# Attention scores over 64 rows of the TensorE array, two head groups issued as a pair, on one Trainium2 core

## Chip, core and metric

The kernel runs on one core of one Trainium2 chip. The metric is the device time in microseconds (us) of one execution. Three timed runs of the kernel before gave a median of 1534.31 us, from 1533.08 to 1535.16. The profile comes from one further execution, which took 1534.36 us.

## What is computed

The reference is a hybrid attention layer followed by a retention and feed-forward layer, on 512 tokens of 1024 features, all in float32. The change touches only the attention of the first layer: a local branch with a window of 128 tokens (8 heads, called A), and a selected and a window branch (8 heads, called B). With 512 tokens the top 16 of 8 blocks are all blocks, so the selected branch is causal attention over everything, and the window of 512 is too. Each branch has 8 query heads of 64 features in two groups; the four heads of a group share one key and one value head:

```python
logits = jnp.einsum('btgrd,bsgd->bgrts', qi, kb) + bias      # d = 64
p = masked_softmax(logits, mask, sink)
return jnp.einsum('bgrts,bsgd->btgrd', p, vb)
```

The compressed branch, the gates, the projections and the second layer are the same before and after.

## The kernel before

`proj` holds the projections with features on the 128 partitions and the 512 tokens along the free dimension. One tile of queries, `proj[:, QA + j]` or `proj[:, QB + j]`, holds two heads: head j of group 0 on partitions 0 to 63 and head j of group 1 on partitions 64 to 127. The keys of a branch lie in the same way, group 0 on the low and group 1 on the high half. A product of queries and keys is taken over all 128 rows. So that the other group adds nothing, the kernel keeps two copies of each key tile with one half set to zero: `k_group0[branch]` has group 0 and zeros on the high half, and the tile in `proj` itself (KA, KS or KW) keeps group 1 with zeros on the low half. These copies are made in VectorE's `head_norm` for t >= 8 (lines 1111 to 1120), with the high halves zeroed at n == 20 (line 1149). KC and VC are tiles whose contents are no longer needed by then; `ka0` is a tile of its own.

The attention is a loop over 96 steps, written out on each engine (`for s in range(STEPS)`; line 1784 on TensorE, 1206 on VectorE, 811 on ScalarE). `Step` gives what step s does: the query block i runs from 0 to 3, in it the branch from 0 to 2, and in that eight heads, j and g with g fastest, so steps s and s+1 with s even are the same j, block and branch, in groups 0 and 1. The width of the scores is 128 times the number of key blocks: i + 1 for the branches 1 and 2, and at most 2 for branch 0. Counting these gives 24 steps of width 128, 40 of 256, 16 of 384 and 16 of 512.

A step goes through the engines like this. TensorE computes the scores of step s into bank s % 2 (called QK(s) below; line 1792). VectorE adds the bias and finds the row's minimum, into `sc[:, s % 2]` (bias(s); line 1217). ScalarE takes the exponential in place (exp(s); line 818). TensorE transposes the result block by block (T(s); line 1817, recorded as line 1571), VectorE for even and ScalarE for odd s copy it out of PSUM (lines 1231, 827), and TensorE multiplies with the values (PV(s); line 1806). On TensorE the order in iteration s of the loop is: wait for bias(s-2), QK(s); PV(s-3); T(s-1), which waits for exp(s-1). VectorE's bias(s) waits for QK(s) and, since it writes `sc[:, s % 2]`, for T(s-2). VectorE also closes each group of eight steps, with its three operations at lines 1241 to 1260.

A float32 product appears in the trace as two instructions LDWEIGHTS and two MATMUL, each with its own weights and both into the same bank; a transpose is one of each. Ahead of the loop lies the computation of the z projections, units n = 16 to 23 (line 1701), with the head norms between, and the compressed branch (lines 1748 to 1781). After the loop TensorE waits for `yl_done` and goes on to the output projection.

Of the kernel before, what the change touches and what calls it, by code (L numbers as in the profile page):

```python
# [28 lines left out]
ALU = mybir.AluOpType  # L29
AX = mybir.AxisListType.X  # L30

P = 128
S = 512
# [5 lines left out]
HD = 64  # L39
# [11 lines left out]
KC, VC, KS, VS, KW, VW, KA, VA, QA, QB, ZA, ZB = 0, 1, 2, 3, 4, 5, 6, 7, 8, 12, 16, 20  # L51
# [46 lines left out]
N_ATT = 8 * N_GROUPS  # L98
# [21 lines left out]
def att(s):  # L120
    return Step(s)


def tail_at(s):

    i, rest = divmod(s - 5, 24)
    return i - 1 if rest == 0 and i > 0 else None
# [36 lines left out]
def hybrid_block(nc, x, c, w_ada, b_ada, norm_gain, w_in, b_nsa_gate, q_gain_a, k_gain_a, sinks,  # L164
# [7 lines left out]
    with ExitStack() as stack:  # L172
# [3 lines left out]
        def sb(name, shape, kb, dt=F32):  # L176
            return nc.alloc_sbuf_tensor_at(name, shape, dt, offset=BASE + int(kb * KB))

        def sem(name):
            return stack.enter_context(nc.semaphore(name))  # L180
# [7 lines left out]
        def const(name, shape, dt=F32):  # L188
            t = sb(name, shape, c_at[0] / KB, dt)
            c_at[0] += (int(np.prod(shape[1:])) * 4 + 31) // 32 * 32  # L190
            return t
# [11 lines left out]
        gains = const("gains", [P, 6])  # L203
# [31 lines left out]
        R = 60  # L235
# [22 lines left out]
        h_hi = sb("h_hi", [P, KT, S], R + 48, F32R)  # L258
        h_lo = sb("h_lo", [P, KT, S], R + 64, F32R)
        proj = sb("proj", [P, 24, S], R + 80)  # L260
        ka0 = sb("k_local_group0", [P, S], R + 128)
        rs_bc = sb("rstd_wide", [P, 2, S], R + 40)
        gb_t = sb("gates_t", [P, S], R + 44)
        hid = sb("cmp_hidden", [P, 2, 64], R + 130.25)
# [71 lines left out]
        ps = nc.alloc_psum_tensor("ps", [P, 8, S], F32)  # L336
# [17 lines left out]
        m = {n: sem(n) for n in names}  # L354
# [1 line left out]

        nrm = {n: sem(n) for n in ("x_done xh_done xl_done xsq_done ss_done nst_mm ms_done rs_done nbc_mm rb_done t_done h_done l_done").split()}


        k_group0 = (ka0[:], proj[:, KC], proj[:, VC])  # L360

        def gate_of(branch):

# [623 lines left out]
        def _(dve):  # L987
            v = nc.vector
            own = Own(dve, m["dve_own"])
# [67 lines left out]
            for u in range(U_KA, U_Z):  # L1057
# [10 lines left out]
                if c is not None:  # L1068
                    dve.wait_ge(ada_in[c], 64 + 16)
                    for k in (2 * c, 2 * c + 1):  # L1070
# [5 lines left out]
                        if k and k % 2 == 0:  # L1076
                            dve.wait_ge(m["adag_done"], c)
                        ins = v.scalar_tensor_tensor(out=acc_g[:], in0=src, scalar=csilu[:, k:k + 1],
                                                     in1=acc_g[:], op0=ALU.mult, op1=ALU.add)
# [26 lines left out]
            def head_norm(t):  # L1106

                dve.wait_ge(m["bc_mm"], t + 1)
                tile = proj[:, NORM_TILES[t]]
                g = NORM_GAINS[t]  # L1110
                if t >= 8:

                    low, high = slice(0, HD), slice(HD, P)
                    own(v.scalar_tensor_tensor(out=k_group0[t - 8][low, :], in0=tile[low, :], scalar=gains[low, g:g + 1],
                                               in1=ps[low, 5 + t % 2], op0=ALU.mult, op1=ALU.mult))
                    v.scalar_tensor_tensor(out=tile[high, :], in0=tile[high, :], scalar=gains[high, g:g + 1],
                                           in1=ps[high, 5 + t % 2], op0=ALU.mult, op1=ALU.mult).then_inc(m["qk_done"], 1)
                    own.wait()
                    own(v.memset(tile[low, :], 0.0))
                    return  # L1120
                v.scalar_tensor_tensor(out=tile, in0=tile, scalar=gains[:, g:g + 1], in1=ps[:, 5 + t % 2],
                                       op0=ALU.mult, op1=ALU.mult).then_inc(m["qk_done"], 1)

# [4 lines left out]
            for n in range(16, 24):  # L1128
                dve_convert(dve, None, 0, n + U_OF + AHEAD)
                if n < 19:  # L1130
                    a, b = NORM_GROUPS[n - 16]
                    dve.wait_ge(m["st_mm"], b)
                    v.tensor_scalar(msq_h[:, 8 * a:8 * b], ps[:, 4, 8 * a:8 * b], EPS, None, ALU.add).then_inc(m["hms_done"], 1)
                if n == 17:
                    cmp_input(1)
                    dve.wait_ge(m["kst_mm"], 1)
                    v.tensor_scalar(kc_ms[0:NC_PAD, :], ps[0:NC_PAD, 7, 448:450], EPS, None, ALU.add).then_inc(m["kms_done"], 1)
                if n == 19:
                    dve.wait_ge(m["kbc_mm"], 1)
                    own(v.memset(kcz[:], 0.0))  # L1140
                    own.wait()
                    for g in range(2):
                        half = slice(g * HD, (g + 1) * HD)
                        v.scalar_tensor_tensor(out=kcz[half, g], in0=kcmp[half, :], scalar=gains[half, 3:4],
                                               in1=ps[half, 7, 480:512], op0=ALU.mult, op1=ALU.mult).then_inc(m["kcmp_done"], 1)
                if n == 20:
                    own(v.memset(vbd[:], 0.0))
                    for k0 in k_group0:
                        own(v.memset(k0[HD:P, :], 0.0))
                for t in BCAST_AT.get(n, ()):  # L1150
                    head_norm(t)
                if n == 22:

                    dve.wait_ge(m["c2_mm"], 2)
                    own.wait()
                    for g in range(2):
                        for j in range(4):
                            part = slice(32 * j, 32 * j + 32)
                            v.tensor_copy(vbd[part, g, j * HD:(j + 1) * HD],
                                          ps[part, 7, 320 + g * HD:384 + g * HD]).then_inc(m["vbd_done"], 1)  # L1160
# [45 lines left out]
            for s in range(STEPS):  # L1206
                if s < N_ATT:
                    u = att(s)
# [16 lines left out]
                t = s - 1  # L1225
# [131 lines left out]
            for t in range(KT):  # L1357
# [6 lines left out]
                for k in MIX_TILES[t]:  # L1364
# [10 lines left out]
                                           op0=ALU.mult, op1=ALU.add))  # L1375
                own.wait()
                own(v.scalar_tensor_tensor(out=conv_t[:], in0=u_pad[:, 2:S + 2], scalar=tap[2], in1=conv_t[:],
                                           op0=ALU.mult, op1=ALU.add))
# [94 lines left out]
            for h in range(RET_HEADS):  # L1473
                for n in range(6):
# [9 lines left out]
                    if n == 5:  # L1484
# [8 lines left out]
                        for t in range(4):  # L1493
                            c1 = V_RET + 4 * h + t
                            own(v.scalar_tensor_tensor(out=val[:], in0=ret[:, 4 * h + t], scalar=col[:, c1:c1 + 1],
                                                       in1=ps[:, 6], op0=ALU.mult, op1=ALU.mult))
# [9 lines left out]
            with dve.Fori(0, 2) as it:  # L1506
                own.begin(it, 4)
                for k in range(8):
                    dve_convert(dve, it, 8, U_YR + k + AHEAD)
                    if k % 2:  # L1510
                        t = k // 2
# [43 lines left out]
            for k in range(3 * KT):  # L1555
                t, part = divmod(k, 3)
# [12 lines left out]
        def _(pe):  # L1569
            def trans(dst, src, parts=P):  # L1570
                return pe.transpose(dst, src, ident[0:parts, 0:parts])  # L1571

            def blk(i):
                return slice(i * P, (i + 1) * P)
# [207 lines left out]


            for s in range(STEPS):
                if s < N_ATT:
                    u = att(s)
                    if s >= 2:
                        pe.wait_ge(m["s_bias"], s - 1)

                    q = (QB if u.branch else QA) + u.j  # L1790
                    keys = proj[:, (KA, KS, KW)[u.branch]] if u.g else k_group0[u.branch]
                    pe.matmul(ps[:, s % 2, 0:u.width], proj[:, q, blk(u.i)],  # L1792
                              keys[:, u.first_block * P:u.first_block * P + u.width],
                              start=True, stop=True).then_inc(m["s_mm"], 1)
                t = s - 3
                if 0 <= t < N_ATT:
                    u = att(t)
                    pe.wait_ge(m["pt_a" if t % 2 else "pt_d"], t // 2 + 1)
                    if t == 0:
                        pe.wait_ge(m["co_done"], NI)  # L1800
                    elif t % 8 == 0 and u.group >= 2:
                        pe.wait_ge(m["comb_done"], u.group - 1)
                    v, blocks = (VA, VS, VW)[u.branch], u.width // P
                    for b in range(blocks):
                        c = (u.first_block + b) * P + u.g * HD
                        mm = pe.matmul(ps[:, 4 + u.group % 2, u.head * HD:(u.head + 1) * HD], pt[:, t % 2, blk(b)],  # L1806
                                       proj[:, v, c:c + HD], start=b == 0, stop=b == blocks - 1)
                    mm.then_inc(m["pv_mm"], 1)
                t = s - 1
                if 0 <= t < N_ATT:  # L1810
                    pe.wait_ge(m["s_exp"], t + 1)
                    if t == 0:
                        pe.wait_ge(m["ctr_mm"], 1)
                    if t >= 2:
                        pe.wait_ge(m["pt_a" if t % 2 else "pt_d"], t // 2)
                    for b in range(att(t).width // P):
                        mm = trans(ps[:, 2 + t % 2, blk(b)], sc[:, t % 2, blk(b)])
                    mm.then_inc(m["t_mm"], 1)
                i = tail_at(s)
                if i is not None:  # L1820
                    pe.wait_ge(m["ob_done"], 2 * i + 2)
                    pe.wait_ge(m["comb_done"], 3 * i + 3)
                    if i:
                        pe.wait_ge(m["yf_done"], 2 * i)
                    for half, o in enumerate((oa, ob[:, i])):
                        for b in range(4):
                            mm = trans(ps[:, 6 + half, blk(b)], o[:, blk(b)])
                    mm.then_inc(m["ytr_mm"], 1)
# [101 lines left out]
            with pe.Fori(0, 2) as it:  # L1930
                for k in range(8):
                    half = k % 2
# [18 lines left out]
            with pe.Fori(0, 2) as it:  # L1951
                for k in range(12):
                    t, part = divmod(k, 3)
# [74 lines left out]
```

## Time and profile before

| | us |
|---|---|
| median of three timed runs | 1534.31 |
| the profiled execution | 1534.36 |
| its span in the trace | 1532.6 |
| TensorE matmul busy | 1481.7 |
| VectorE busy | 744.9 |
| ScalarE busy | 576.0 |
| GpSimd busy | 85.7 |
| the attention loop, from its first to its last score or transpose | about 245.9 to 377.9 |

Times in the trace count from the start of the span, which is 1.8 us shorter than the execution. PE is the matmul side of TensorE and PEld its weight loads. The start of a matmul is recorded; its end is modelled and takes in the way through the array, so neighbouring matmuls overlap in the rows and the distance of two starts tells what one costs in a stream.

### The profile page before, as it was taken

What the parts mean: (1) busy time and instruction counts of PE and PEld (TensorE: products, weight loads), DVE (VectorE), ACT (ScalarE), POOL (GpSimd) and SP (SyncE); (2) the same over time, 40 slices, a digit from 0 to 9 for tenths busy, and PEclk for the clock granted to TensorE, in tenths of its full rate; (3) what the DMA queues carried; (4) which work ended last, traced back from release to release, by engine and by line L of the source; (5) the groups of instructions that cost most, each with busy time, mean ns of one, the idle gap of its engine ahead of it and who ended that gap; (6) DMA issues with size and microseconds to landing.
All of it is one profiled execution on the core that took longest, in us unless ns stands there. A gap on an engine that the chain in (4) does not pass through costs nothing.

```text
span 1532.6 us, 18206 instructions
## 1 busy us (share of the span) xinstructions
PE 1481.7 (97%) x7006; PEld 1233.1 (80%) x7006; DVE 744.9 (49%) x1205; ACT 576.0 (38%) x949; POOL 85.7 (6%) x90
## 2 busy tenths in 40 slices
PE   5899997998999999999999999999999999999998
PEld 4688886887888888888888878878878888888886
DVE  5743156875556653454544525554456533333332
ACT  3432335654433333233333334442345433333221
POOL 1110400000000000001000022210000000000000
PEclk9997899999999999999999999999999999999998
DMA  7992310000252333322221223225333323232321
GB/s 230 277 267 73 107 56 15 2 1 1 83 165 86 107 105 96 100 84 68 70 83 56 82 60 93 83 83 165 92 88 94 107 87 109 87 106 87 113 76 55
DMA packets 227757, 145.51 MB, mean 95 GB/s; under 512 B 6082, under 2 KB 216250, under 8 KB 227424
## 3 DMA queue, kind: packets, MB, share of 16 engines
q1 hardware_dynamic: 224784, 131.90, 29.6%
q0 software_dynamic: 2896, 12.57, 2.9%
q8 instruction: 50, 0.82, 0.2%
q14 instruction: 27, 0.22, 0.0%
HBM read 138.82 MB, written 4.59 MB: 94 GB/s over the span
## 4 chain that ended last, share of the span: by engine, by line
PE 69%; issue 24%; DVE 3%; SPq 2%; ACT 1%; DMA 0%; POOLq 0%; POOL 0%; DVEq 0%; ACTq 0%
PE ps L381 44%; PE ps L1872 6%; PE ps L1896 3%; PE ps L1670 3%; PE ps L1792 3%; PE ps L1571 3%; PE ps L1806 3%; PE ps L1882 1%; PE ps L1693 1%; SPq L479 1%; PE ps L1686 1%; SPq L501 1%; SPq L515 1%; DMA w_raw<-in_w_in_dram 0%; PE ps L1780 0%
## 5 line engine op out<-in xcount | busy, mean ns | idle before, releaser
L399 DVE TENSOR_TENSOR w_lo<-w_raw,w_hi 128x1024 fp32r<-128x1024 f32 (+1 forms) x215 | 261.2, 1218 | 245.4 <-ACT w_hi L394 242.7
L394 ACT ACTIVATE w_hi<-w_raw 128x1024 fp32r<-128x1024 f32 (+1 forms) x215 | 220.4, 1034 | 24.2 <-PE ps L381 12.8
L431 ACT ACTIVATE temps<-ps 128x512 f32<-128x512 f32 x68 | 40.6, 597 | 251.1 <-PE ps L381 251.1
L381 PE MATMUL ps<-g_hi,w_hi 128*128 128x512 f32 x384 | 97.4, 396 | 0.0
L381 PE MATMUL ps<-g_hi,w_lo 128*128 128x512 f32 x384 | 94.9, 389 | 0.0
L381 PE MATMUL ps<-g_lo,w_hi 128*128 128x512 f32 x384 | 94.8, 389 | 0.0
L381 PEld LDWEIGHTS ps<-g_hi,w_hi 128*128 128x128 f32 x384 | 71.6, 188 | 16.4 <-issue 1.9
L381 PEld LDWEIGHTS ps<-g_hi,w_lo 128*128 128x128 f32 x384 | 72.1, 188 | 15.1
L381 PEld LDWEIGHTS ps<-g_lo,w_hi 128*128 128x128 f32 x384 | 72.1, 188 | 15.0
L1806 PEld LDWEIGHTS ps<-proj,probs_t 128*128 128x128 f32 x432 | 61.4, 191 | 13.9 <-issue 7.6
L818 ACT ACTIVATE scores_sb<-scores_sb,row_min 128x256 f32<-128x256 f32 (+3 forms) x96 | 51.2, 533 | 54.3 <-DVE row_min L1217 53.3
L381 PE MATMUL ps<-f_hi,w_hi 128*128 128x512 f32 x288 | 71.1, 389 | 0.0
L381 PE MATMUL ps<-f_hi,w_lo 128*128 128x512 f32 x288 | 71.1, 389 | 0.0
L381 PE MATMUL ps<-f_lo,w_hi 128*128 128x512 f32 x288 | 71.1, 389 | 0.0
L381 PEld LDWEIGHTS ps<-f_hi,w_lo 128*128 128x128 f32 x288 | 54.1, 188 | 11.2
L381 PEld LDWEIGHTS ps<-f_hi,w_hi 128*128 128x128 f32 x288 | 54.1, 188 | 11.2
L381 PEld LDWEIGHTS ps<-f_lo,w_hi 128*128 128x128 f32 x288 | 54.1, 188 | 11.2
L1806 PE MATMUL ps<-proj,probs_t 128*128 128x64 f32 x432 | 58.6, 263 | 0.0
L1792 PE MATMUL ps<-proj 128*128 128x256 f32 (+3 forms) x160 | 53.8, 418 | 0.0
L628 POOL TENSOR_TENSOR rstd<-mean_squares,minus_half 128x4 f32<-128x4 f32 x8 | 8.2, 1023 | 766.4 <-DVE mean_squares L1300 733.0
L1282 DVE TENSOR_TENSOR x_t<-temps,x_t 128x512 f32<-128x512 f32 x16 | 11.1, 692 | 81.9 <-ACT temps L431 81.9
L1571 PE MATMUL ps<-ident,scores_sb 128*128 128x128 f32 x224 | 42.8, 284 | 6.3 <-ACT scores_sb L818 6.0
(368 smaller groups left out, 2740.1 us busy)
## 6 DMA issues: line engine op xcount, KB each, us to landing
w_raw<-in_w_in_dram SPq DMA_DIRECT2D x107, 512.0 KB, 3.8
w_raw<-in_w_ff_gate_dram SPq DMA_DIRECT2D x22, 512.0 KB, 3.8
w_raw<-in_w_ff_up_dram SPq DMA_DIRECT2D x22, 512.0 KB, 3.8
w_ada_shift_scale<-in_w_ada_dram SPq DMA_DIRECT2D x16, 512.0 KB, 6.7
w_raw<-in_w_r_out_dram SPq DMA_DIRECT2D x16, 512.0 KB, 4.6
w_raw<-in_w_ff_down_dram SPq DMA_DIRECT2D x16, 512.0 KB, 4.2
w_ada_gate<-in_w_ada_dram SPq DMA_DIRECT2D x4, 1024.0 KB, 9.2
w_raw<-in_w_out_dram SPq DMA_DIRECT2D x8, 512.0 KB, 4.0
```

Of the source, the lines that this page charges most:

```text
L381: mm = pe.matmul(bank, w[:, slot, k], mov[:, at_k], start=first and n == 0 and k == 0, stop=last and n == 2 and k == kts - 1)
L394: act.activation(whi[:, slot, 0:kts], raw[:, slot, 0:kts], ACT.Copy).then_inc(hi_done, 1)
L399: nc.vector.tensor_tensor(wlo[:, slot, 0:kts], raw[:, slot, 0:kts], whi[:, slot, 0:kts].bitcast(F32), ALU.subtract).then_inc(lo_done, 1)
L431: act.activation(dst, ps[:, o % 4], func, scale=scale).then_inc(evac, 1)
L479: sp.dma_start(ada[:, u % 4, :, part], w_ada_v[:, :, n:n + P]).then_inc(ada_in[u % 4], 16)
L818: a.activation(sc[:, s % 2, 0:w], sc[:, s % 2, 0:w], ACT.Exp, scale=-1.0, bias=row_min[:, G % 2, n:n + 1], accum_out=den[:, G % 2, att(s). ...
L1571: return pe.transpose(dst, src, ident[0:parts, 0:parts])
L1670: mm = pe.matmul(ps[:, 4 - 4 * q + j], half_rows(w, u)[:, kk, blk(j)], h[:, 2 * c2 + kk], start=c2 == 0 and n == 0 and kk == 0, stop=c2 == ...
L1792: pe.matmul(ps[:, s % 2, 0:u.width], proj[:, q, blk(u.i)], keys[:, u.first_block * P:u.first_block * P + u.width], start=True, stop=True). ...
L1806: mm = pe.matmul(ps[:, 4 + u.group % 2, u.head * HD:(u.head + 1) * HD], pt[:, t % 2, blk(b)], proj[:, v, c:c + HD], start=b == 0, stop=b = ...
L1872: mm = pe.matmul(ps[:, 4 + j], x[:, 2 * c2 + kk, blk(j)], half_rows(w, u)[:, kk], start=c2 == 0 and n == 0 and kk == 0, stop=c2 == 3 and n ...
L1896: mm = pe.matmul(ps[:, 4 + t], w[:, j, blk(t)], p[:, j], start=n == 0 and j == 0, stop=n == 2 and j == NI - 1)
```

## The change

The key tiles are no longer split: `head_norm` handles them as it handles the query tiles, with one operation over 128 partitions, and the copies, their zeroing and the tile `ka0` go away. The score products now take only the 64 partitions of their group, for queries and keys. On TensorE the scores of steps s and s+1 are issued one right after the other at the even s, each behind its wait for the bias two steps before it; at odd s none are issued.

```diff
-        ka0 = sb("k_local_group0", [P, S], R + 128)
-        k_group0 = (ka0[:], proj[:, KC], proj[:, VC])
...
-                if t >= 8:
-
-                    low, high = slice(0, HD), slice(HD, P)
-                    own(v.scalar_tensor_tensor(out=k_group0[t - 8][low, :], in0=tile[low, :], scalar=gains[low, g:g + 1],
-                                               in1=ps[low, 5 + t % 2], op0=ALU.mult, op1=ALU.mult))
-                    v.scalar_tensor_tensor(out=tile[high, :], in0=tile[high, :], scalar=gains[high, g:g + 1],
-                                           in1=ps[high, 5 + t % 2], op0=ALU.mult, op1=ALU.mult).then_inc(m["qk_done"], 1)
-                    own.wait()
-                    own(v.memset(tile[low, :], 0.0))
-                    return
                 v.scalar_tensor_tensor(out=tile, in0=tile, scalar=gains[:, g:g + 1], in1=ps[:, 5 + t % 2],
                                        op0=ALU.mult, op1=ALU.mult).then_inc(m["qk_done"], 1)
...
                     own(v.memset(vbd[:], 0.0))
-                    for k0 in k_group0:
-                        own(v.memset(k0[HD:P, :], 0.0))
...
             for s in range(STEPS):
-                if s < N_ATT:
-                    u = att(s)
-                    if s >= 2:
-                        pe.wait_ge(m["s_bias"], s - 1)
-
-                    q = (QB if u.branch else QA) + u.j
-                    keys = proj[:, (KA, KS, KW)[u.branch]] if u.g else k_group0[u.branch]
-                    pe.matmul(ps[:, s % 2, 0:u.width], proj[:, q, blk(u.i)],
+                for e in (s, s + 1) if s < N_ATT and s % 2 == 0 else ():
+                    u = att(e)
+                    if e >= 2:
+                        pe.wait_ge(m["s_bias"], e - 1)
+
+                    q, half = (QB if u.branch else QA) + u.j, slice(u.g * HD, u.g * HD + HD)
+                    keys = proj[half, (KA, KS, KW)[u.branch]]
+                    pe.matmul(ps[:, e % 2, 0:u.width], proj[half, q, blk(u.i)],
                               keys[:, u.first_block * P:u.first_block * P + u.width],
                               start=True, stop=True).then_inc(m["s_mm"], 1)
```

## Rows read from the trace of the kernel before

**Rows 1.** The page's busy time of each engine: us, share of the span, instructions.
```profile
PE 1481.7 (97%) x7006; PEld 1233.1 (80%) x7006; DVE 744.9 (49%) x1205; ACT 576.0 (38%) x949; POOL 85.7 (6%) x90
```

**Rows 2.** Stretches of the loop: length, busy of PE, PEld, DVE, ACT, POOL, clock, DMA.
```profile
250.00:262.00 12.00, 9.72 (x76) 8.44 (x76) 7.69 (x45) 8.07 (x40) 0.00 (x0) 1.00 0.01 3
...
344.00:358.00 14.00, 14.00 (x92) 10.65 (x89) 7.31 (x20) 7.63 (x18) 0.00 (x0) 1.00 0.01 2
```

**Rows 3.** Timeline of PE: start, length, engine, line, operation; scores of neighbouring steps.
```profile
289.01 0.60 PE L1792 MATMUL ps<-proj 128*128 128x256 f32 x2
290.06 0.60 PE L1792 MATMUL ps<-proj 128*128 128x256 f32 x2
...
346.33 1.02 PE L1792 MATMUL ps<-proj 128*128 128x512 f32 x2
348.47 1.02 PE L1792 MATMUL ps<-proj 128*128 128x512 f32 x2
```

**Rows 4.** Timeline, single instructions of one step of width 512, on PE.
```profile
350.51 0.27 PE L1571 MATMUL ps<-ident,scores_sb 128*128 128x128 f32 x1
350.62 0.59 PE L1792 MATMUL ps<-proj 128*128 128x512 f32 x1
351.05 0.59 PE L1792 MATMUL ps<-proj 128*128 128x512 f32 x1
```

**Rows 5.** Timeline of a narrow step (width 128), from one stalled transpose to the next.
```profile
249.27 0.33 PE L1571 MATMUL ps<-ident,scores_sb 128*128 128x128 f32 x1 [0.38 <-ACT scores_sb L818]
249.43 0.39 PE L1792 MATMUL ps<-k_local_group,proj 128*128 128x128 f32 x2
249.86 0.35 DVE L1217 CUSTOM_DVE_ANT_0 scores_sb<-ps,band_a,sinks_negated 128x128 f32<-128x128 f32 x1
250.25 0.40 ACT L818 ACTIVATE scores_sb<-scores_sb,row_min 128x128 f32<-128x128 f32 x1 [0.49 <-DVE row_min L1217]
250.80 0.33 PE L1571 MATMUL ps<-ident,scores_sb 128*128 128x128 f32 x1 [0.26 <-ACT scores_sb L818]
```

**Rows 6.** Timeline around two products on a part of the array, ahead of the loop.
```profile
76.32 0.26 PE L1571 MATMUL ps<-ident,vec 110*128 110x110 f32 x1
76.51 0.14 PEld L1571 LDWEIGHTS ps<-ident,vec 32*128 32x128 f32 x1 [0.28 <-issue]
...
190.69 0.39 PE L381 MATMUL ps<-h_lo,w_hi 128*128 128x512 f32 x1
191.01 0.10 PEld L1571 LDWEIGHTS ps<-ident,k_compressed_rstd 32*64 32x64 f32 x1 [0.35 <-issue]
191.01 0.21 PE L1571 MATMUL ps<-ident,k_compressed_rstd 32*64 32x32 f32 x1
191.15 0.13 PEld L1581 LDWEIGHTS ps<-ident,k_compressed_rstd 32*64 32x64 f32 x1
191.23 0.22 PE L1581 MATMUL ps<-ident,k_compressed_rstd 32*64 32x32 f32 x1
191.37 0.15 PEld L1571 LDWEIGHTS ps<-ident,rstd_wide 128*128 128x128 f32 x1
```

**Rows 7.** Timeline: a float32 product whose weights could not be loaded ahead.
```profile
240.62 0.19 PEld L1780 LDWEIGHTS ps<-v_compressed_diagonal,probs_t 128*128 128x128 f32 x1 [2.19 <-issue]
240.65 0.45 PE L1780 MATMUL ps<-v_compressed_diagonal,probs_t 128*128 128x256 f32 x1 [1.98 <-DVE probs_t L1192]
240.94 0.38 PE L1780 MATMUL ps<-v_compressed_diagonal,probs_t 128*128 128x256 f32 x1
```

**Rows 8.** Timeline of DVE: what the split of one key tile costs.
```profile
218.28 0.74 DVE L1114 SCALAR_TENSOR_TENSOR k_local_group<-proj,gains,ps 64x512 f32<-64x512 f32 x1 [10.98 <-PE ps L1571]
219.06 0.75 DVE L1116 SCALAR_TENSOR_TENSOR proj<-proj,gains,ps 64x512 f32<-64x512 f32 x1
219.97 0.48 DVE L1119 MEMSET proj<- 64x512 f32 x1 [0.16 <-issue]
```

**Rows 9.** Waits from 180 to 246 us: the only one of PE for DVE.
```profile
PE ps L1780 <- DVE probs_t L1192: 2.0, 1, 2.0
```

## The prediction

> **What bounds the kernel now.** I read the page's engine totals first: TensorE is busy for 97% of the span [rows 1], so the question is whether it is also full where the change acts. The change acts in the attention loop, 132 of 1534 us. The stretches of the loop show two regimes [rows 2]: with blocks of scores 512 wide, PE is busy for 14.00 of 14.00 us; with blocks 128 wide, for 9.72 of 12.00 us.
>
> In the full regime the distance of the score products is the cost of a step: 1.05 us at width 256 and 2.14 at 512 [rows 3]. Within a step, a score instruction of width 512 starts 0.43 us before the next, so the two of a product take 0.86, and a transpose takes 0.11 [rows 4]. That is the rate of all of it: an instruction takes its width x 0.43/512 us, but not under 0.11, which is what its load of 128 columns of weights takes. A product of width w so costs 0.21 us per 128 columns; width 256: scores 0.43, four value instructions 0.43, two transposes 0.21, sum 1.07 against 1.05 seen.
>
> In the narrow regime a chain sets the pace [rows 5]: transpose 249.27, scores 249.43, bias 249.86, exponential 250.25, next stalled transpose 250.80: 1.53 us for two steps, with PE waiting at its end for ScalarE.
>
> **The change part by part.** *Split of the keys.* For each of three key tiles VectorE loses 0.74 + 0.75 + 0.48 and gains one operation over 128 partitions, which takes as long as one over 64 at the same width, say 0.74 [rows 8]; with three fills of 0.48 that is 3 x 1.23 + 1.4 = 5 us less of VectorE's work between 195 and 229 us. I cost it at nothing: the one wait of PE for VectorE in that stretch is 2.0 us for another operation, at 240.6, which follows from products of PE that end after these [rows 9]. If that cover were missing, it could give at most those 5 us.
>
> *Where the halves of the array could save.* By the code, 12 pairs of steps have width 128, 20 have 256, 8 have 384 and 8 have 512. A score product keeps its width, so over 64 rows it costs the same 0.21 us per 128 columns; what can be won is overlap of the two groups. No row shows two products side by side. The ends are no overlap (four units of the cost of one instruction per pair, as now) and full overlap (two units). I take three, for this reason: each product is two MATMULs with their own weights on the same rows, so the two of one group can't overlap, and in all rows MATMULs start in the order of the program. Then group 1's first can start with group 0's second at the earliest, and its second is alone. One unit of four is saved: per pair 0.21 at 256, 0.32 at 384, 0.43 at 512. At 128 I count nothing, since four weight loads of 0.11 fill that time anyway. Over the pairs in the full regime: 20 x 0.21 + 8 x 0.32 + 8 x 0.43 = 10.2 us.
>
> *What switching costs.* All else in the loop uses the whole array, so each pair enters and leaves another shape of it. The rows of three such entries and exits agree [rows 6]. The first weight load of the new shape starts 0.07 us before the modelled end of the matmul before it and no earlier: 76.32 + 0.26 - 0.07 = 76.51; 190.69 + 0.39 - 0.07 = 191.01; and out, 191.23 + 0.22 - 0.08 = 191.37. In one shape it is loaded during the matmul before. A float32 product with weights not loaded ahead begins late by that load: 240.94 less its cost of 0.21 is 240.73, or 0.11 us after the load at 240.62 [rows 7]. In: from the last transpose's start 0.27 - 0.07 + 0.11 = 0.31 instead of 0.11, so 0.20 more [rows 4]. Out: the last score instruction takes 0.59 by its row where it costs 0.43 [rows 4]; 0.59 - 0.07 + 0.11 = 0.63 instead of 0.43, again 0.20. A round trip is 0.40 us. The nearest lower bound is the trip at 76 us, about 0.27, where the load is that of a transpose; the lowest is zero, if 64 rows are not such a shape. The Trainium skill, page "TensorEngine Tiling (Array Packing)", section "Key Properties", says that a change of tiling mode drains TensorE; the trace agrees, with the 0.32 us from 190.69 to 191.01.
>
> In the full regime 36 trips cost 36 x 0.40 = 14.4. In the narrow one the chain passes only through the entry (transpose, then scores); the exit falls in the time in which PE waits for the exponential. 12 x 0.20 = 2.4.
>
> *Order and waits.* Scores of s+1 now come ahead of PV(s-3) and T(s-1), behind the wait for bias(s-1). Queued behind that wait are those two, and ScalarE and VectorE wait for them. bias(s-1) waits for T(s-3), which ends well before: at width 256, from there to QK(s+1) PE has PV 0.43, T 0.21, the entry 0.20 and QK(s) 0.43, 1.27 us in all, for one bias. Closing a group may delay one in eight a little, as it does now. The other chain, from the end of QK(s) to T(s), has 0.43 + 0.21 + 0.43 + 0.43 = 1.50 us of PE work now and 0.21 + 0.20 + 0.43 + 0.21 + 0.43 = 1.48 after. I cost the order at nothing; what hides it is that PE work, and at width 256 it has little to spare.
>
> **The sum**, against the profiled execution of 1534.36 (the median, 1534.31, is the same): + 14.4 + 2.4 - 10.2 = + 6.6 us, 1541.0. By width, in us a pair: + 0.20 at 128, + 0.19 at 256, + 0.08 at 384, - 0.03 at 512.
>
> **Rivals.**
> *A, the switch is free* (64 full-width rows are no new shape, or the drain needs nothing). Then only the 10.2 us remain: 1524.2, faster. Against it: three entries and exits of three shapes all drained. For it: none of them was 64 x 128. It decides the sign where a round trip costs under 10.2 / 42 = 0.24 us (36 full trips and 12 halves), and 0.27 is the lowest seen.
> *B, full overlap* (two units). Saves 20.5 instead of 10.2, with the switch as forecast: 1530.7. Against it: the order of MATMULs and the two of each product.
> *C, no overlap*: four units as now, with the switch: 1534.4 + 16.8 = 1551.2. For it: the trace shows no two products at once, ever.
> *D, each half drains too*: going from one part of the array to another, the load at 191.15 came 0.21 - 0.07 = 0.14 after the matmul at 191.01, where 0.05 would do, though the shape was the same [rows 6]. Then there is no overlap, and per full pair one more drain of 0.20: 1551.2 + 36 x 0.20 = 1558.4. For it: that row; against it: there both parts shared their rows, here they don't. The Trainium skill, page "TensorE: Matmul & The Clock Gate", section "The mechanism", says that weight loads overlap with matmuls in flight only on other rows, and that matmuls start in order. By the first, this rival would fall and the forecast's overlap stand; no row shows either half of it for these halves.
>
> **How the numbers follow.** Forecast 1541 with chance 0.45 (its own range 1537 to 1545, for a trip between 0.31 and 0.50 us), A 0.13, B 0.10, C 0.17, D 0.10, and 0.05 for something else, such as a lower clock: the loop's stretches had 1.00 even where PE was busy for only 9.72 of 12 us [rows 2]. The range for 8 in 10 leaves out A and the unnamed rest: from 1529, below B, to 1560, above D. About 0.2%, or 3 us, is what a measurement of this kernel can tell from no change. Faster by more: A, half of B and a little of the rest, 0.20. Within: half of B, and the forecast's case with a trip near the low bound of 0.27, 0.14. Slower: 0.66.
>
> **What would show it.** In the timeline after, the first weight load of a pair stands about 0.20 us behind the last transpose's start, and that of the values 0.52 behind the last score instruction at width 512; if they are pulled ahead, A holds. The start of group 1's first MATMUL equals that of group 0's second if there is overlap, that of group 0's first if B holds, and lies a unit behind it for C. A pair at 512 takes 4.26 us (now 4.28), at 256 about 2.3 (now 2.1), at 128 about 1.73 (now 1.53). The stage ahead of the loop keeps its length though VectorE is busy 5 us less. Idle time of PE at width 256 that ends with the exponential or the bias would mean that the order costs after all; a clock under 1.00 in the loop would break all of it.

## The result

The changed kernel takes 1541.11 us (median of 20 runs), the kernel before 1535.14 (20 runs): a ratio of 1.0046, 95% interval 1.0030 to 1.0061. That ratio is one of means, over all but the slowest run of the changed kernel: two of its twenty took 1561.54 and 1563.29, with an average clock of 0.954 where the others have 0.969 to 0.972. The medians alone give 1.0039, or 6.0 us more. I had forecast 6.6 more, 1541.0. The number is right, but two terms of its sum were wrong and cancelled, which is luck: the overlap of the two halves saves two of the four units of a pair and not one, and in the profiled run the clock of TensorE fell for 30.7 us, which I had given a small chance.

### The profile after

In the changed kernel the scores are line 1777, the values 1791, the transposes 1556, bias 1202, exponential 815. The engine totals of its page (us, share of the span, instructions) answer to [rows 1]:

```profile
span 1539.3 us, 18197 instructions
PE 1490.7 (97%) x7006; PEld 1226.6 (80%) x7006; DVE 740.1 (48%) x1196; ACT 577.6 (38%) x949; POOL 85.6 (6%) x90
```

VectorE does 4.8 us less, in 9 instructions fewer, as the removed copies should give; PE is busier by 9 us. The stretches of the loop (columns as in [rows 2]) show where:

```profile
250.00:262.00 12.00, 11.65 (x61) 9.05 (x60) 6.47 (x34) 7.09 (x31) 0.00 (x0) 0.60 0.01 2
262.00:274.00 12.00, 11.94 (x54) 8.85 (x55) 6.45 (x32) 6.87 (x27) 0.00 (x0) 0.50 0.00 1
284.00:296.00 12.00, 11.49 (x85) 8.42 (x84) 9.03 (x34) 8.46 (x29) 0.00 (x0) 1.00 0.00 0
358.00:372.00 14.00, 14.00 (x102) 10.29 (x102) 8.62 (x22) 7.60 (x18) 0.00 (x0) 1.00 0.01 2
```

The column before the last two is the granted clock. It is 0.50, the 1.2 GHz level, at 262 to 274 us, and 1.00, 2.4 GHz, from 284 us on. PE "busy" for 11.94 of 12 us there did only 54 matmuls. In the kernel before, the clock is 1.00 both at 250 to 262 us [rows 2] and in the stretch after it, with 75 matmuls:

```profile
262.00:274.00 12.00, 10.64 (x75) 9.51 (x76) 9.06 (x33) 7.05 (x28) 0.00 (x0) 1.00 0.01 1
```

The loop starts at 246.2 us, before at 245.9: the stage ahead of it keeps its length, as forecast.

The score products on PE, in starts of pairs (start, length, instructions merged), answer to [rows 3]:

```profile
248.25 0.49 PE L1777 MATMUL ps<-proj 64*128 64x128 f32 x4
249.97 0.49 PE L1777 MATMUL ps<-proj 64*128 64x128 f32 x4
251.70 0.49 PE L1777 MATMUL ps<-proj 64*128 64x128 f32 x4
...
255.68 0.81 PE L1777 MATMUL ps<-proj 64*128 64x128 f32 x4
257.80 0.84 PE L1777 MATMUL ps<-proj 64*128 64x128 f32 x4
...
294.61 0.70 PE L1777 MATMUL ps<-proj 64*128 64x256 f32 x4
296.84 0.70 PE L1777 MATMUL ps<-proj 64*128 64x256 f32 x4
...
362.61 1.13 PE L1777 MATMUL ps<-proj 64*128 64x512 f32 x4
366.43 1.13 PE L1777 MATMUL ps<-proj 64*128 64x512 f32 x4
```

A narrow pair takes 1.73 us at the high clock and 2.12 at the low one (1.53 before), a pair of width 256 takes 2.23 (2.10), and one of width 512 takes 3.82 (4.28). These are the usual pairs; a pair at which VectorE closes a group of eight steps takes longer (289.86 to 292.39, 2.53 us at width 256). Inside the pair at 362.61, looked at in slices short enough to keep its instructions apart, as [rows 4]:

```profile
362.41 0.27 PE L1556 MATMUL ps<-ident,scores_sb 128*128 128x128 f32 x1
362.61 0.19 PEld L1777 LDWEIGHTS ps<-proj 64*128 64x128 f32 x2 [0.17 <-issue]
362.61 0.70 PE L1777 MATMUL ps<-proj 64*128 64x512 f32 x2
363.15 0.59 PE L1777 MATMUL ps<-proj 64*128 64x512 f32 x1
363.67 0.19 PEld L1791 LDWEIGHTS ps<-proj,probs_t 128*128 128x128 f32 x1 [0.76 <-issue]
```

The entry is as forecast: the first weight load stands 0.20 us behind the last transpose's start. So is the exit: the values' load stands 0.52 behind the last score instruction. But at 362.61 there are two weight loads and two MATMULs, one of each half of the rows: in the trace neither of the two MATMULs signals the end of a product, and both at 363.15 do, so they are the first and the second of each product. The two products run side by side from the first instruction.

### The profile page after: what moved, and what is told of

Same layout as the page of the kernel before. It is cut to its first block, busy times and chain, and to the rows that moved or that the text cites. A ratio compares the mean times of both kernels' runs of the same rounds, so it can differ in the third digit from the quotient of the medians.

```text
span 1539.3 us, 18197 instructions
## 1 busy us (share of the span) xinstructions
PE 1490.7 (97%) x7006; PEld 1226.6 (80%) x7006; DVE 740.1 (48%) x1196; ACT 577.6 (38%) x949; POOL 85.6 (6%) x90
## 4 chain that ended last, share of the span: by engine, by line
PE 70%; issue 24%; DVE 3%; ACT 1%; DMA 1%; SPq 0%; POOLq 0%; POOL 0%; DVEq 0%; ACTq 0%
PE ps L378 44%; PE ps L1857 6%; PE ps L1791 3%; PE ps L1556 3%; PE ps L1881 3%; PE ps L1655 3%; PE ps L1777 2%; PE ps L1867 1%; PE ps L1678 1%; PE ps L1620 1%; PE ps L1671 1%; DMA x_tok<-in_x_dram 1%; DMA w_raw<-in_w_in_dram 0%; PE ps L1765 0%; DVE ada_sum L1003 0%
## 5 line engine op out<-in xcount | busy, mean ns | idle before, releaser
L1791 PE MATMUL ps<-proj,probs_t 128*128 128x64 f32 x432 | 69.1, 290 | 0.0
L1556 PE MATMUL ps<-ident,scores_sb 128*128 128x128 f32 x224 | 46.4, 301 | 4.2 <-ACT scores_sb L815 4.1
L378 PE MATMUL ps<-x_gain_hi,w_hi 128*128 128x512 f32 x192 | 47.8, 390 | 0.0
```

What stands on the lines that cost most here:

```text
L378: mm = pe.matmul(bank, w[:, slot, k], mov[:, at_k], start=first and n == 0 and k == 0, stop=last and n == 2 and k == kts - 1)
```

## The experiments

All but the fillers' kernels are built on the kernel before with its padded copies kept, which hold both forms: over 128 rows as before, or the low 64 rows of the one copy and the high 64 of the other. There the scores are line 1800. The diffs show what each edit comes to, with conditions that are constant in it worked out. The kernel before took 1535.48, 1535.14 and 1535.11 us beside the three groups of runs.

### The order alone

```diff
-                if s < N_ATT:
-                    u = att(s)
+                for e in (s, s + 1) if s < N_ATT and s % 2 == 0 else ():
+                    u = att(e)
...
+                    half = slice(0, P)
```

> Before, with the scores of steps s and s+1 issued together, but over all 128 rows with the padded key copies. Theory: the order costs only where its chain is longer than the work of PE that covers it, about 0.12 us a pair at width 256 (2.22 us in the kernel after against 2.10 with the switch and full overlap), 20 pairs, so + 2.4 us against before, 1537.5, and the clock stays at 1.00 in the loop, because it is the 64-row products that let it fall. Rival: the order alone, with its longer pauses between bursts, lets the clock fall at about 252 us as in the kernel after; then about + 8 us more, 1545.

Measured: 1536.08 us, ratio 1.0000 (0.9991 to 1.0009), every run with the average clock of before, 0.98.

```profile
285.25 1.03 PE L1800 MATMUL ps<-proj 128*128 128x256 f32 x4
287.35 1.03 PE L1800 MATMUL ps<-proj 128*128 128x256 f32 x4
...
355.34 1.88 PE L1800 MATMUL ps<-proj 128*128 128x512 f32 x4
359.62 1.88 PE L1800 MATMUL ps<-proj 128*128 128x512 f32 x4
```

The order costs nothing as long as the pair keeps its four units: 2.10 and 4.28 us a pair, as before, and 121.88 us from the first scores to those of the last pair, where before has 121.89. The 2.4 us that I expected of it were wrong for this kernel; they belong to the shorter pair (below). And the clock isn't let fall by the order.

### 64 rows, each product alone

```diff
-                    keys = proj[:, (KA, KS, KW)[u.branch]] if u.g else k_group0[u.branch]
-                    pe.matmul(ps[:, s % 2, 0:u.width], proj[:, q, blk(u.i)],
+                    half = slice(u.g * HD, u.g * HD + HD)
+                    keys = proj[half, (KA, KS, KW)[u.branch]] if u.g else k_group0[u.branch][half, :]
+                    pe.matmul(ps[:, s % 2, 0:u.width], proj[half, q, blk(u.i)],
```

> Before, with products over 64 rows (padded copies kept, their zero halves not read), each alone in its own step: the order of before, twice as many entries and exits, no overlap. Theory: 72 round trips of 0.40 us where PE is full are + 28.8 us, the 24 narrow steps add 5 to 10 us as their chain passes two round trips, and if 64-row products let the clock fall, 8 us or more on top: 1569 to 1585, with the clock at 0.50 in the narrow part. Rival, the switch is free and the gain comes from 64 rows as such: 1535 or less.

Measured: four runs, 1579.93, 1647.39, 1649.44 and 3850.23 us. Only the first lies in the range that I expected. Since they lie so far apart, I take only the profile, which is of the run of 1647.39. Its clock is at 0.50 for 195 us of the loop; the steps of width 512 run after that at 1.00:

```profile
250.00:262.00 12.00, 12.00 (x40) 8.56 (x40) 4.08 (x22) 4.86 (x21) 0.00 (x0) 0.50 0.01 2
...
444.00:456.00 12.00, 12.00 (x61) 6.87 (x60) 8.34 (x23) 6.62 (x18) 0.00 (x0) 1.00 0.00 0
```
```profile
454.77 1.12 PE L1800 MATMUL ps<-proj 64*128 64x512 f32 x2
457.30 1.12 PE L1800 MATMUL ps<-proj 64*128 64x512 f32 x2
```

A step takes 2.53 us where before has 2.14 [rows 3]: 0.39 for a round trip, with the 0.40 of the forecast. The switch is not free, and one such product alone is a loss. What made one run take 3850 us, with an average clock of 1.00, I didn't find.

### Both products on the low half

Against the kernel after with the copies kept:

```diff
-                    half = slice(u.g * HD, u.g * HD + HD)
+                    g = 0
+                    half = slice(g * HD, g * HD + HD)
```

> The kernel after, with copies kept, and both products of a pair on the low 64 rows (the second group repeats the first's scores, so its heads are computed from the wrong scores). The same shapes, order and switches; only the overlap is impossible. Theory of full overlap (two of four units saved): 20 x 0.43 + 8 x 0.64 + 8 x 0.85 = 20.5 us more than the kernel after, 1561.6, and the four MATMULs of a pair start one unit apart. Rival, one unit saved as I forecast: 10.2 us more, 1551. Rival, no overlap in the kernel after: the same 1541.

Measured: 1562.17 us, ratio 1.0173 (1.0157 to 1.0189).

```profile
293.98 1.13 PE L1800 MATMUL ps<-proj 64*128 64x256 f32 x4
296.47 1.13 PE L1800 MATMUL ps<-proj 64*128 64x256 f32 x4
299.00 1.13 PE L1800 MATMUL ps<-proj 64*128 64x256 f32 x4
...
379.14 1.98 PE L1800 MATMUL ps<-proj 64*128 64x512 f32 x4
383.81 1.98 PE L1800 MATMUL ps<-proj 64*128 64x512 f32 x4
```
```profile
374.46 0.69 PE L1800 MATMUL ps<-proj 64*128 64x512 f32 x1
375.00 0.59 PE L1800 MATMUL ps<-proj 64*128 64x512 f32 x1
375.43 0.59 PE L1800 MATMUL ps<-proj 64*128 64x512 f32 x1
```

On one half the four MATMULs follow one another: 0.54 us behind the first, then 0.43, a unit, each. A pair of 512 takes 4.67 us: 0.39 above the pairs of the order alone, again the round trip, and 0.85 above the kernel after, two units of 0.43. That is full overlap. At 256 the usual pair takes 2.49, 0.39 above the order alone, but only 0.26 above the kernel after, where two units would be 0.43. That the total met the 1561.6 is again luck. The scores of the last pair come 146.89 us behind the first, 19.05 more than in the kernel after; 12.85 of these arise from the seventeenth pair on, where both kernels are at the high clock, and 6.20 ahead of it, where this kernel stays at the low clock for 37.5 us instead of 30.7. So the overlap is worth less than the 20.5 that I expected, and the low clock adds what is missing.

### The copies kept

Against the kernel after, and with VectorE's copies and fills left in:

```diff
-                    keys = proj[half, (KA, KS, KW)[u.branch]]
+                    keys = proj[half, (KA, KS, KW)[u.branch]] if u.g else k_group0[u.branch][half, :]
```

> The kernel after with VectorE's key copies and fills kept (the pairs read the low half of one copy and the high half of the other). Theory: the 5 us of VectorE's work were hidden, the same time as after, 1541.1 within 1. Rival: they were not, up to 5 us more.

Measured: 1542.55 us, ratio to before 1.0039 (1.0025 to 1.0052), an interval that takes in the 1.0046 of the kernel after. The 5 us of VectorE's work were hidden; the copies' removal gives at most a part of the 1.4 us between the medians.

### A filler in the narrow part

```diff
+                if s % 2 == 1 and 3 <= s < 24:
+                    pe.matmul(ps[:, 7, 0:P], ident[:], ident[:], start=True, stop=True)
                 t = s - 1
                 if 0 <= t < N_ATT:
                     pe.wait_ge(m["s_exp"], t + 1)
```

> The kernel after with one more product per pair in the narrow part (steps 3 to 23, odd): the identity times itself over all 128 rows, 0.21 us, into a bank that nothing else uses there, placed where PE waits for the exponential. It computes nothing that is used. Theory: the fall of the clock (0.50 from 252.4 to 283.1 us in the kernel after) comes from too little work of the array in the narrow part; with the filler it stays at 1.00, the narrow pairs take 1.73 us instead of 2.12 (9 of them, 3.5 us) and the four pairs of width 256 that ran at 0.50 take about 10.4 us instead of 14.5 (4.1 us): 1541.1 - 7.6 = 1533.5. Rival: the clock falls because of the switches as such, whatever fills the pauses: it falls as before, and the time is 1541 or more.

Measured: twelve runs in two groups. Seven have an average clock of 0.980 to 0.983 and take 1531.5 to 1535.4, median 1534.5; five have 0.966 to 0.968 and take 1547.9 to 1548.8. In the profile of one of the first group:

```profile
250.00:262.00 12.00, 11.54 (x84) 8.64 (x84) 7.35 (x39) 7.48 (x37) 0.00 (x0) 1.00 0.01 2
```

The usual pairs there take 1.66 us, less than the 1.73 without the filler, so it does a little more than keep the clock; I didn't find why. With the clock kept, the kernel after would stand at about 1534.5, level with the kernel before: the fall of the clock costs it some 6.6 us. But the filler keeps it only in some runs, and in the others the time is 7 us above that of the kernel after, at a lower average clock than its 0.972.

### Pairs over halves for the wide scores only

```diff
-                if s < N_ATT:
-                    u = att(s)
+                if s >= N_ATT:
+                    now = ()
+                elif att(s).width >= 384:
+                    now = (s, s + 1) if s % 2 == 0 else ()
+                else:
+                    now = (s,)
+                for e in now:
+                    u = att(e)
...
+                    half = slice(g * HD, g * HD + HD) if att(e).width >= 384 else slice(0, P)
```

> Before, with pairs over row halves only for the 16 pairs of width 384 and 512 and the products of before for all narrower ones (the padded copies hold both forms). Theory: full overlap less a round trip of 0.40 us gives 0.24 us a pair at 384 and 0.46 at 512, 5.6 us in all, and the clock stays at 1.00: 1529.8 where before has 1535.4. Rival: some of it is lost at the eight borders between the two orders, or the clock falls in the wide part: no gain, 1535 or more.

Measured: 1530.93 us, ratio 0.9974 (0.9966 to 0.9983), all eleven runs with a clock of 0.98. This kernel is faster than both.

```profile
312.46 0.92 PE L1800 MATMUL ps<-proj 64*128 64x384 f32 x4
315.41 0.92 PE L1800 MATMUL ps<-proj 64*128 64x384 f32 x4
...
352.32 1.13 PE L1800 MATMUL ps<-proj 64*128 64x512 f32 x4
356.14 1.13 PE L1800 MATMUL ps<-proj 64*128 64x512 f32 x4
```

A pair of 384 takes 2.95 (3.19 by four units), one of 512 takes 3.82 (4.28). That is 5.6 us by this count, and 4.2 by the medians. The count takes all pairs for usual ones, and where a group is closed or the width changes part of the gain is lost.

### Pairs over halves from the second block on

The edit is that of the last kernel with `att(s).i >= 1` in place of the width.

> Before, with pairs over row halves from the second block of queries on (all widths from 256), the first block as before. Theory: the narrow part keeps the clock; then the pairs of width 256 lose 0.12 us each by their chain (2.4 us) and the wide ones gain 5.6: 1532.2. Rival: at width 256 the half-row pairs let the clock fall by themselves; then some 4 us or more on top, 1536 or more, with a stretch at 0.50 behind 266 us.

Measured: 1531.51 us, ratio 0.9982 (0.9973 to 0.9990), eleven runs with a clock of 0.98. The narrow part over 128 rows keeps the clock, and then the pairs of 256 keep it too. The only thing that it does differently from the kernel after is that first block (and the copies), and that is worth 9.6 us by the medians, or 11.0 against the kernel after with the copies kept: up to 2.4 for its entries and about 7 for the clock, which leaves up to 2 open. The pairs of 256 cost less than the 2.4 us that I expected of them: from the first scores to those of the last pair there are 119.14 us, and 117.78 with pairs over halves for the wide scores only; the medians differ by 0.6.

### Switches without half rows

On the kernel with the order alone:

```diff
+                if s % 2 == 0 and 2 <= s < 24:
+                    pe.matmul(ps[:, 7, 0:32], ident[0:32, :], ident[0:32, 0:32], start=True, stop=True)
```

> The paired order over all 128 rows (padded copies), with one small product over 32 rows and 32 columns behind each pair of the narrow part, whose result is not used: it brings an entry and an exit per pair, in the time in which PE waits anyway, while the scores keep all rows. Theory that the 64-row products are what is too little for the clock: it stays at 1.00 and the time is that of the paired order, 1536, or up to 2 more. Rival, that the two switches per pair are what lets it fall: 0.50 from about 252 us on and some 4 to 8 us more.

Measured: 1538.17 us, ratio 1.0019 (1.0010 to 1.0029), ten runs with an average clock of 0.979 to 0.982. The clock didn't fall:

```profile
250.00:262.00 12.00, 11.81 (x80) 9.51 (x78) 6.54 (x38) 8.22 (x35) 0.00 (x0) 1.00 0.01 2
```

Two switches a pair and the paired order are there, the scores have all rows, and the clock stays. Most of the narrow pairs take 1.80 to 1.86 us, so this trip is not all hidden behind the wait. The small product also gives PE some work more, so that the switches by themselves would let the clock fall isn't fully excluded.

### Low, low, high

On the kernel with the copies kept:

```diff
                     u = att(e)
+                    if e % 2 and 82 <= e:
+                        pe.wait_ge(m["yf_done"], 6)
+                        low = proj[0:HD, QB + u.j, blk(u.i)]
+                        pe.matmul(ps[:, 7], low, k_group0[u.branch][0:HD, :], start=True, stop=True)
```

> The kernel after with copies kept; in seven of the eight pairs of width 512 one more product on the low half between the two of the pair, its result not used. The order of the program is then low, low, high. Theory: each row half works through its own instructions, whatever stands before them in the program: the first MATMUL of the high half starts with the first of the pair (within 0.02 us), two products ahead of its place, and a pair takes 3.82 + 0.85 = 4.67 us. Rival: a MATMUL can pass only the one before it: then the high half's first starts 0.8 us or more behind the pair's first.

Measured, in one run of 1562.75 us whose clock was at 0.50 from 249 to 328 us, ahead of these pairs (slices of PE's timeline; line 1804 is the pair, 1796 the added product):

```profile
376.96 0.71 PE L1804 MATMUL ps<-proj 64*128 64x512 f32 x2
377.50 0.60 PE L1804 MATMUL ps<-proj 64*128 64x512 f32 x2
377.92 0.59 PE L1796 MATMUL ps<-proj 64*128 64x512 f32 x1
...
381.63 1.14 PE L1804 MATMUL ps<-proj 64*128 64x512 f32 x4
```

Both halves of the pair start at 376.96, and the added product, which stands between them in the program, begins at 377.92, 0.41 us behind the start of the high half's second MATMUL. A pair takes 4.67 us, four units on the low half and no more. The first theory holds: the halves don't wait for each other.

### Two fillers

As the filler above, with two products of 0.21 us.

> The kernel after with two full-row products of 0.21 us per pair in the narrow part instead of the one of the earlier run, where five of twelve runs still showed the lower clock. Theory: what the array gets to do in the narrow part decides; with two fillers all runs keep the clock (0.98 on average over the span) and take 1532 to 1537. Rival: it is chance in each run whatever is added: again some near 1548.

Measured: ten runs, five with an average clock of 0.981 or 0.982 at 1532.1 to 1534.6, five with 0.965 or 0.966 at 1551.8 to 1553.2, slower still than with one filler. The expectation fell: more filler doesn't keep the clock more often.

## Why the prediction was right, and where it was not

| term | forecast, us | measured, from the usual pair, us |
|---|---|---|
| round trips, 36 pairs | + 14.4 | 36 x 0.39 = + 14.0 |
| entries in the narrow chain, 12 | + 2.4 | 12 x (1.73 - 1.53) = + 2.4 |
| overlap | - 10.2 | - 20 x 0.26 - 8 x 0.63 - 8 x 0.85 = - 17.0 |
| clock | 0 | + 7 |
| removed work of VectorE | 0 | 0 to - 1.4 |
| sum | + 6.6 | about + 6; by the medians + 6.0 |

The last column multiplies the usual pair by the number of pairs, which is too much for single terms. The nineteenth pair, of width 256 and one of those at which a group is closed, takes 2.53 us in all three forms: over all rows (280.62 to 283.15 with the order alone), on one half (296.47 to 299.00) and on two (289.86 to 292.39); the twenty-seventh takes 3.46 in all three. There neither the trip nor the overlap shows. Whole stretches, from the start of one pair's scores to that of another's, give it without this error:

| kernel, us | pairs 1 to 17 | pairs 17 to 48 |
|---|---|---|
| before | 29.69 | 92.21 |
| order alone | 29.69 | 92.19 |
| after | 38.89 | 88.96 |
| after with the filler, clock kept | 31.60 | 88.96 |
| both products on the low half | 45.09 | 101.81 |

Behind the seventeenth pair the round trips cost 101.81 - 92.19 = 9.6 us, where 31 usual pairs would make 12.1, and the overlap gives 101.81 - 88.96 = 12.9, where they would make 15.2. The difference of the two is the same either way, - 3.2 and - 3.1, and that is what the total rests on. Ahead of the seventeenth pair the kernel after loses 9.2 us to the order alone, 7.3 of them the difference to the filler's run and so the clock's.

**The switch held** for the usual pair, to a few hundredths: entry, exit, and 0.39 against 0.40 in two experiments. The forecast's count of it, 36 and 12 times, was too high, since the pairs that close a group don't show it. Its + 2.4 in the narrow chain rests on two pairs ahead of the fall of the clock. The rule taken from three small products ahead of the loop (the load starts 0.07 us before the modelled end of the last matmul) carried over to a shape that no row had shown. Rival A is out.

**The overlap was mis-sized**, and by a wrong step: "in all rows MATMULs start in the order of the program". That was true of the rows, all of which had one stream of instructions on one shape of the array. On the two halves, group 1's first MATMUL starts 0.01 us after group 0's first and half a microsecond ahead of group 0's second, and low-low-high shows it passing a whole product more. It was rival B, to which I gave 0.10, though the time came out 10 us above B's 1530.7. The Trainium skill, page "TensorE: Matmul & The Clock Gate", section "The mechanism", says that matmuls start and end strictly in the program's order; these runs show starts in another order for two halves of the rows, and the measurement decides (the ends are modelled). Rivals C and D are out with it: the halves need no drain between them.

**At width 256 part of the gain was lost to a chain**, which the forecast had costed at nothing with the remark that there was little to spare. The 1.48 us of PE's work that had to cover the chain were counted with three units; with two they are 0.21 us less. The timeline of the kernel after shows one pair:

```profile
292.39 0.70 PE L1777 MATMUL ps<-proj 64*128 64x256 f32 x4
293.12 0.43 DVE L1202 CUSTOM_DVE_ANT_0 scores_sb<-ps,band_b 128x256 f32<-128x256 f32 x1 [0.20 <-PE ps L1777]
293.59 0.51 ACT L815 ACTIVATE scores_sb<-scores_sb,row_min 128x256 f32<-128x256 f32 x1 [0.87 <-DVE row_min L1202]
294.24 0.44 PE L1556 MATMUL ps<-ident,scores_sb 128*128 128x128 f32 x2
294.61 0.30 PEld L1777 LDWEIGHTS ps<-proj 64*128 64x128 f32 x4 [0.17 <-DVE row_min L1202]
```

Scores, bias, exponential, transpose of the same step, next pair: 2.22 us, the pair's period. ScalarE and VectorE wait for PE and PE for them; the chain has become the bound, with 0.17 of the 0.43 us lost in it (2.49 - 2.23 = 0.26 gained). In the kernel with the order alone the same chain fits into the pair's 2.10.

**The clock was the rest.** I put it into the unnamed 0.05, with the row that showed 1.00 at 9.72 of 12 us busy [rows 2] as a reason against it. That row had products over all rows. In the kernel after, the clock went to 0.50 from 252.4 to 283.1 us. From 253.56 to 270.65, eight narrow pairs took 17.1 us, and 14.1 in the filler's profile; the next four, of width 256, took 14.5, and 10.3 in the kernel that pairs from the second block on. Together 7.2, near the 6.6 by the filler's runs. It fell in the runs of the kernels with 64-row scores in the narrow part and no filler (20 of the kernel after, 4 with both products on one half, 5 with the copies kept, one low-low-high, and three of the four with each product alone, all but that of 3850 us, whose average is 1.00), and in none of the 43 with scores over 128 rows there, though these include the paired order, a switch per pair, and half rows from width 256 on. For the runs without a profile this goes by their average clock: 0.979 to 0.983 in the 43, at most 0.972 in the others. So the 64-row products in the narrow part bring it about. The order isn't needed for it, nor is the overlap, since it also fell with each product alone and with both on one half; the order isn't enough either, and the switches weren't. PE's busy time just ahead of the fall doesn't tell these cases apart: of the 4 us from 248 on it was busy for 3.13 in the kernel after, and with the clock kept for 3.14 with the order alone and for 2.65 with pairs from the second block on. What about the 64-row products the clock responds to is open: the fillers gave PE more full-row work in the same time, and it fell in about half of the runs all the same.

## What to carry to other kernels

Products over 64 rows pay in pairs on the two halves of the array, when they are wide enough that half of a pair's time is clearly more than the 0.39 us of leaving the full shape and coming back, here from width 384 on (0.24 us a pair; the pairs of 256 only broke even on PE's side, 2.10 - 0.43 + 0.39 = 2.06 against 2.10, and lost to the chain behind them). Keep the full-row form where the stretch is bound by a chain anyway: there the switch lengthens the chain, and the clock may fall. And when a forecast comes out right, check its terms: here an error of some 7 us in switch and overlap together cancelled one of 7 us in the clock, and only the terms showed the version that beats both kernels.

## What the runs showed that I had not expected

- Two row halves are served independently, weight loads and MATMULs alike: the later product of the program started 0.01 us behind the earlier one, ahead of the earlier one's second MATMUL, and with one more product between them ahead of that too.
- Entry and exit of the 64-row shape cost 0.20 us each, and the first load stands 0.07 us before the modelled end of the last MATMUL, as for the 32-row shapes in [rows 6]. Moving between the halves leaves no trace in the time: 4.28 less two units of 0.43, plus 0.39, is 3.81, and a pair of 512 takes 3.82.
- The clock fell to 1.2 GHz at 252.4 us in the kernel after, where PE had been busy for 3.13 of the 4 us from 248 on, and stayed at 2.4 GHz in the kernel before, with 3.35 of 4 in the same stretch. It came back after 30.7 us in the profile of the kernel after, and after 78.5 in that of low-low-high, which has the same narrow part.
